# A 512-column matmul over both halves of the activations in three wide up projections

## The chip, the cores and the metric

The program runs on one core of a Trainium2 chip. Its time is the device time of one execution in microseconds (us). TensorE (PE in the profile) multiplies, ScalarE (ACT) and VectorE (DVE) do the elementwise work, GpSimd (POOL) does a few small powers and loads, and the DMA queue of SyncE (SP) brings in the weights.

## The reference, cut to what matters

Two blocks of a transformer, for 256 tokens of width 1024, in float32. Three of their layers are wide; they are the ones that change.

```python
def squared_relu_mlp(h, w_up, w_down):          # w_up 1024 x 4096, w_down 4096 x 1024, once
    return jnp.square(jax.nn.relu(h @ w_up)) @ w_down

def conv_ffn(h, up, conv_w, conv_b, down):      # up 1024 x 5632, down 2816 x 1024, in two layers
    u = causal_depthwise_conv(h @ up, conv_w, conv_b)      # width 3, along the tokens
    g, val = jnp.split(u, 2, axis=-1)
    return (jax.nn.silu(g) * val) @ down
```

## The kernel before, in words

**Split numbers.** Each float32 matrix is kept as two float32r matrices, a high half (the value rounded, `whi`, `h_hi`, `r_hi`) and a low half (the value minus the high half, `wlo`, `h_lo`, `r_lo`). A product is three matmuls into one PSUM region: high by high, high by low, low by high (`three`, L1860 to L1862).

**Units.** The weights come in 203 units of at most 1 MB in the order of use, through five slots. SyncE loads unit u once unit u-5 has been used. ScalarE makes its high half (`hi()`, L737), VectorE its low half (`lo()`, L1144), and TensorE waits for the low half in `weights(u)`.

**Wide layers.** The hidden dimension is cut into groups of 256 columns, 16 in the squared-ReLU layer (called MLP below) and 11 in each convolution layer (FFN below). An MLP group has one up unit (1024 x 256) and one down unit (256 x 1024). An FFN group has two up units, x = 0 for the gate and x = 1 for the value, and one down unit. The up product is made transposed, with the weights as the stationary operand and the activations as the moving one: for each of 2 column blocks c and 8 row blocks k, three matmuls with 256 columns (the tokens). Both column blocks of a unit share one PSUM bank. A down unit is 24 matmuls with 512 columns, with the activations stationary; it accumulates over all groups into banks 4 to 7.

**Order on TensorE.** In the MLP: up 0, up 1, down 0, up 2, down 1, and so on to down 15. In each FFN: group 0's up product in another form with the tokens on the partitions (`first_half`, `first_back`), then both units of up 1, down 0, up 2, down 1, ..., up 9, up 10, down 8, and downs 9 and 10 together (`last_two_wide`: for each of 4 output banks first the 6 matmuls of down 9, then the 6 of down 10). So the up units of groups 9 and 10 follow each other, four in a row. TensorE waits for `up_lo` (MLP) or `f_lo` (FFN) of the group before its down unit; both are given by VectorE's subtraction that makes `r_lo` (L1536, L1715).

**Order on ScalarE and VectorE.** Their programs are written out by hand, and each engine takes its instructions in that order. For an FFN group g of 1 or more:

```python
# ScalarE
hi(); ffn_first(g, 0)    # 2 Identity with scale and bias (L998), then Copy to the padded buffer (L1000)
hi(); ffn_first(g, 1)
ffn_silu(g); hi(); ffn_part(g)          # L1004, L737, L1008: r_hi
# VectorE
lo(); ffn_taps(g, 0)     # waits for the Copy, then 4 scalar_tensor_tensor (L1701)
lo(); ffn_taps(g, 1)
ffn_prod(g); lo(); ffn_part(g)          # L1710, L1144, L1715: r_lo, gives f_lo
```

Group 0 has no `hi()` in it and only the first two `lo()`. For an MLP group ScalarE does Relu (L900), Square (L902) and the high half (L904), VectorE only `r_lo` (L1536), each with its `hi()` or `lo()` around it.

**Banks.** A bank may be written again only when it has been drained; here that is the inc that ScalarE's reading instruction gives. Up units turn through banks 0, 1, 2 (MLP) and 0 to 3 (FFN).

Of the kernel before, what the change touches and what calls it, by code (L numbers as in the profile page):

```python
# [33 lines left out]
F32 = mybir.dt.float32  # L34
F32R = mybir.dt.float32r
# [172 lines left out]
def plan(w):  # L208
# [100 lines left out]
    def mlp_up(g):  # L309
        p.unit(("up", g), w["w_up"][0], 0, KD, 256 * g, 256)  # L310
        p.gemm(("up", g), ("up", g), g % 3)

# [53 lines left out]
    def ffn(layer, name, sum_banks, first_banks):  # L366
        p.tile_transposes(name, sum_banks)
        up, down = w["ffn_up_2"][layer], w["ffn_down_2"][layer]

        def ffn_up(g):  # L370
            for x in range(2):
                p.unit(("fu", layer, g, x), up, 0, KD, FFN * x + 256 * g, 256)
                if g:
                    p.gemm(("fu", layer, g, x), ("fu", layer, g, x), 2 * (g % 2) + x)
# [73 lines left out]
def build(nc, w, out):  # L448
# [3 lines left out]
    with ctx:  # L452
# [10 lines left out]
        whi = [sb(f"whi{i}", [P, UNIT], F32R) for i in range(SLOTS)]  # L463
        h_hi, h_lo = sb("h_hi", [P, KD, T], F32R), sb("h_lo", [P, KD, T], F32R)
        r_hi, r_lo = sb("r_hi", [P, KD, T], F32R), sb("r_lo", [P, KD, T], F32R)
# [83 lines left out]

        bank = [ctx.enter_context(nc.psum_tensor(f"bank{i}", [P, 512], F32)) for i in range(8)]  # L550

# [21 lines left out]
        xa_max, xa_p, up_sq = sem("xa_max"), sem("xa_p"), sem("up_sq")  # L573
        f_conv, f_silu, f_prod = (sem(n) for n in ("f_conv", "f_silu", "f_prod"))
        dt_log, dta_ready, cum_row = sem("dt_log"), sem("dta_ready"), sem("cum_row")
# [144 lines left out]
        def _(act):  # L720
# [267 lines left out]
            def ffn_first(layer, g, x):  # L988

                p_ = g % 2  # L990
                key = ("fu", layer, g, x)
                b = wait_bank(act, key)
                if x == 0 and g >= 2:
                    act.wait_ge(f_lo, 11 * layer + g - 1)
                for ct in range(2):
                    tile = FFN_TILES * x + 2 * g + ct
                    wcol, bcol = 128 + 132 * layer + 88 + tile, 392 + 44 * layer + tile
                    A(fcv[p_][x][:, ct, :], b[:, T * ct:T * ct + T], ACT.Identity, scale=pv[:, wcol:wcol + 1],  # L998
                      bias=pv[:, bcol:bcol + 1])
                A(fpad[p_][x][:, :, 2:2 + T], pair(b), ACT.Copy).then_inc(drained[use[key][0]], 1)  # L1000

# [124 lines left out]
        def _(dve):  # L1126
            V = nc.vector
            steps, parts, nxt, powers = [0], [0], [0], [0]

            def mark(ins):  # L1130
# [562 lines left out]
            def ffn_taps(layer, g, x):  # L1693
                key = ("fu", layer, g, x)
# [149 lines left out]
        def _(pe):  # L1844
# [350 lines left out]
            def mlp_first():  # L2195

                w_hi, w_lo, kt, n = weights(at[("up", 0)])
                b = claim(("up", 0))
                for half in range(2):
                    for c in range(2):  # L2200
                        for k in range(4 * half, 4 * half + 4):
                            if c == 0 and k % 2 == 0:
                                wait_drained(pe, ("h3", k // 2))
                            cs = slice(P * c, P * c + P)
                            last = three(b[:, T * c:T * c + T], w_hi[:, k, cs], w_lo[:, k, cs], h_hi[:, k, :], h_lo[:, k, :],
                                         (c, k) == (0, 0), (c, k) == (1, kt - 1))
                        if (half, c) == (0, 0):
# [3 lines left out]
            def mlp_up(g):  # L2211
                if g == 0:
                    mlp_first()
                else:
                    b_unit(at[("up", g)], h_hi, h_lo, one(("up", g)))

# [125 lines left out]
            def ffn(layer, name, before_last):  # L2342
# [46 lines left out]
                for n, (what, g) in enumerate(FFN_ORDER):  # L2389
                    if what == "up":  # L2390
                        for x in range(2):
                            key = ("fu", layer, g, x)
                            b_unit(at[key], h_hi, h_lo, one(key), between=up_second if (g, x) == (1, 0) else None)
                    elif g < FFN_GROUPS - 2:
# [191 lines left out]
```

## Time and profile before

| | |
|---|---|
| time, median of 3 runs | 1349.54 us (1348.79 to 1351.38) |
| the profiled execution | 1347.98 us, span 1346.2 us |
| TensorE busy | 1294.0 us, 96% of the span |
| VectorE busy | 884.4 us, 66% |
| ScalarE busy | 675.5 us, 50% |
| chain that ended last | TensorE 86%, VectorE 7%, ScalarE 3% |
| mean granted TensorE clock | 0.994 |
| HBM read | 219.91 MB |

A busy share says how much of the span an engine worked; the chain says which work set the end. The durations of single instructions include their latency, and neighbours overlap, so the cost of one more instruction is read from the distance of the starts of two neighbours. The unit boundaries are seen on SyncE's queue: it issues a load as soon as TensorE has finished a unit.

### The profile page before, as it was taken

What the parts mean: (1) busy time and instruction counts of PE and PEld (TensorE: products, weight loads), DVE (VectorE), ACT (ScalarE), POOL (GpSimd) and SP (SyncE); (2) the same over time, 40 slices, a digit from 0 to 9 for tenths busy, and PEclk for the clock granted to TensorE, in tenths of its full rate; (3) what the DMA queues carried; (4) which work ended last, traced back from release to release, by engine and by line L of the source; (5) the groups of instructions that cost most, each with busy time, mean ns of one, the idle gap of its engine ahead of it and who ended that gap; (6) DMA issues with size and microseconds to landing.
All of it is one profiled execution on the core that took longest, in us unless ns stands there. A gap on an engine that the chain in (4) does not pass through costs nothing.

```text
span 1346.2 us, 20023 instructions
## 1 busy us (share of the span) xinstructions
PE 1294.0 (96%) x8543; PEld 1177.6 (87%) x8543; DVE 884.4 (66%) x1174; ACT 675.5 (50%) x844; POOL 53.8 (4%) x62
## 2 busy tenths in 40 slices
PE   6999999999999999989999999899999899899997
PEld 6878999988979999989998777899998877899996
DVE  5665757775446444467876777676668757676667
ACT  3555434444435444446674443455555463555552
POOL 4000000100000000000000000000000100000000
PEclk9999999999999999989999999999999999999999
DMA  9644555655435555545552233555554532555551
GB/s 338 196 125 132 182 157 169 226 184 197 163 94 185 188 188 188 164 142 179 168 183 95 94 116 113 179 188 188 188 188 135 179 126 94 188 175 185 184 184 56
DMA packets 155241, 222.26 MB, mean 165 GB/s; under 512 B 4997, under 2 KB 117377, under 8 KB 155024
## 3 DMA queue, kind: packets, MB, share of 16 engines
q1 hardware_dynamic: 151936, 210.38, 48.2%
q0 software_dynamic: 2928, 10.00, 2.0%
q8 instruction: 68, 1.11, 0.3%
q10 hardware_dynamic: 288, 0.59, 0.1%
q14 instruction: 21, 0.17, 0.0%
HBM read 219.91 MB, written 1.05 MB: 164 GB/s over the span
## 4 chain that ended last, share of the span: by engine, by line
PE 86%; DVE 7%; ACT 3%; issue 2%; DMA 1%; POOL 1%; POOLq 0%; DVEq 0%; SPq 0%; ACTq 0%
PE bank L1860 26%; PE bank L1861 26%; PE bank L1862 26%; DVE wlo L1144 1%; ACT whi L737 1%; DMA raw<-in_w_in 1%; POOL rstd L646 1%; PE bank L2280 1%; PE bank L2281 1%; PE bank L2140 1%; PE bank L1952 1%; PE bank L2027 0%; PE bank L2161 0%; DVE bn L1260 0%; ACT h_hi L746 0%
## 5 line engine op out<-in xcount | busy, mean ns | idle before, releaser
L1144 DVE TENSOR_TENSOR wlo<-raw,whi 128x2048 fp32r<-128x2048 f32 (+2 forms) x203 | 454.3, 2247 | 120.5 <-ACT whi L737 120.1
L1860 PE MATMUL bank<-h_hi,whi 128*128 128x256 f32 x1568 | 448.5, 286 | 8.2 <-DVE wlo L1144 5.1
L1861 PE MATMUL bank<-h_lo,whi 128*128 128x256 f32 x1568 | 446.2, 285 | 0.0
L1862 PE MATMUL bank<-h_hi,wlo 128*128 128x256 f32 x1568 | 446.1, 285 | 0.0
L737 ACT ACTIVATE whi<-raw 128x2048 fp32r<-128x2048 f32 (+2 forms) x203 | 379.2, 1881 | 25.4 <-DMA raw<-in_w_in 12.8
L1860 PEld LDWEIGHTS bank<-h_hi,whi 128*128 128x128 f32 x1568 | 303.5, 194 | 11.1 <-DVE wlo L1144 8.5
L1861 PEld LDWEIGHTS bank<-h_lo,whi 128*128 128x128 f32 x1568 | 303.6, 194 | 1.2
L1862 PEld LDWEIGHTS bank<-h_hi,wlo 128*128 128x128 f32 x1568 | 303.4, 194 | 0.0
L1860 PE MATMUL bank<-whi,r_hi 128*128 128x512 f32 (+1 forms) x464 | 180.1, 388 | 3.9 <-DVE wlo L1144 1.4
L1861 PE MATMUL bank<-wlo,r_hi 128*128 128x512 f32 (+1 forms) x464 | 178.3, 384 | 0.0
L1862 PE MATMUL bank<-whi,r_lo 128*128 128x512 f32 (+1 forms) x464 | 178.0, 384 | 0.0
L1701 DVE SCALAR_TENSOR_TENSOR arena<-arena,pv 128x256 f32<-128x256 f32 x176 | 77.5, 482 | 96.8 <-ACT arena L1000 95.2
L1860 PE MATMUL bank<-whi,h_hi 128*128 128x512 f32 (+4 forms) x320 | 117.0, 366 | 1.3 <-issue 0.9
L1861 PE MATMUL bank<-wlo,h_hi 128*128 128x512 f32 (+4 forms) x320 | 114.2, 357 | 0.0
L1862 PE MATMUL bank<-whi,h_lo 128*128 128x512 f32 (+4 forms) x320 | 114.2, 357 | 0.0
L1860 PEld LDWEIGHTS bank<-whi,r_hi 128*128 128x128 f32 x464 | 87.4, 188 | 20.9 <-issue 3.5
L754 ACT ACTIVATE arena<-bank 128x512 f32<-128x512 f32 (+3 forms) x81 | 43.3, 558 | 122.8 <-PE bank L1862 109.5
L998 ACT ACTIVATE arena<-bank,pv 128x256 f32<-128x256 f32 x88 | 44.9, 562 | 117.5 <-PE bank L1862 112.5
L1862 PEld LDWEIGHTS bank<-whi,r_lo 128*128 128x128 f32 x464 | 87.2, 188 | 17.6
L1861 PEld LDWEIGHTS bank<-wlo,r_hi 128*128 128x128 f32 x464 | 87.4, 188 | 15.1
L1860 PEld LDWEIGHTS bank<-whi,h_hi 128*128 128x128 f32 x320 | 60.8, 190 | 10.2 <-issue 2.6
L1862 PEld LDWEIGHTS bank<-whi,h_lo 128*128 128x128 f32 x320 | 60.9, 190 | 8.5
(296 smaller groups left out, 1356.1 us busy)
## 6 DMA issues: line engine op xcount, KB each, us to landing
raw<-in_ffn_up SPq DMA_DIRECT2D x44, 1024.0 KB, 5.1
raw<-in_w_in SPq DMA_DIRECT2D x32, 1024.0 KB, 5.8
raw<-in_ssd_in_proj SPq DMA_DIRECT2D x24, 1024.0 KB, 5.4
raw<-in_ffn_down SPq DMA_DIRECT2D x22, 1024.0 KB, 4.9
raw<-in_w_up SPq DMA_DIRECT2D x16, 1024.0 KB, 5.4
raw<-in_w_down SPq DMA_DIRECT2D x16, 1024.0 KB, 4.8
raw<-in_w_xkv SPq DMA_DIRECT2D x8, 1024.0 KB, 5.1
raw<-in_ssd_out_proj SPq DMA_DIRECT2D x8, 1024.0 KB, 5.0
```

What stands on the lines that cost most here:

```text
L646: nc.gpsimd.tensor_tensor(rstd[:, t:t + 1], ms[:, t:t + 1], mhalf[:, t:t + 1], ALU.pow).then_inc(rstd_ready, 1)
L737: A(whi[u % SLOTS][:, 0:kt * n], raw[u % SLOTS][:, 0:kt * n], ACT.Copy).then_inc(hi_split, 1)
L754: A(dst, src(b), ACT.Copy).then_inc(drained[use[key][0]], 1)
L998: A(fcv[p_][x][:, ct, :], b[:, T * ct:T * ct + T], ACT.Identity, scale=pv[:, wcol:wcol + 1], bias=pv[:, bcol:bcol + 1])
L1144: V.tensor_tensor(wlo[s][:, 0:kt * n], raw[s][:, 0:kt * n], whi[s][:, 0:kt * n].bitcast(F32), ALU.subtract).then_inc(lo_split, 1)
L1701: ins = V.scalar_tensor_tensor(y, fpad[g % 2][x][:, ct, tap:tap + T], pv[:, wcol:wcol + 1], y, ALU.mult, ALU.add)
L1860: M(o, a_hi, b_hi, start=start, stop=False)
L1861: M(o, a_hi, b_lo, start=False, stop=False)
L1862: return M(o, a_lo, b_hi, start=False, stop=stop_)
L1952: last = nc.tensor.transpose(b[:, P * k:P * k + P], xn[:, t, P * (4 * c + k):P * (4 * c + k) + P], ident)
L2140: last = M(b[:, T * t:T * t + T], qT[:, 2 * i + kk, P * t:P * t + P], kT[:, 2 * i + kk, :], start=kk == 0, stop=kk == 1)
L2280: M(b[:, 0:TRI], pick[:, h:h + 1].to_broadcast([2 * SSD_HEADS, P]), crow2[:, :], start=True, stop=False)
```

## The change

In the up units of the three layers (all 16 in the MLP, those of groups 1 to 10 in each FFN) the two halves of the activations lie behind each other in one buffer `h_both`, and a matmul with the high half of the weights takes both, as 512 columns: columns 0 to 255 of the bank get high by high, columns 256 to 511 high by low. The third product, low by high, stays a 256-column matmul into columns 0 to 255. Each column block now fills a bank of its own, two banks per unit. ScalarE copies the upper half of both banks out (`low_copy`), VectorE adds the lower half of each bank to it (`add_halves`) and gives the banks free. In the FFN, ScalarE's Identity instructions come after that and read SBUF; VectorE's taps wait for them (`f_last`). In the MLP, ReLU and square are one `scalar_tensor_tensor` on VectorE. Group 0 of each FFN keeps its product; there ScalarE copies first and its Identity instructions read the copy.

```diff
+            def both(b, w_hi_k, w_lo_k, k, kt):          # TensorE
+                if k == 0:
+                    M(b[:, :], w_hi_k, h_both[:, :, k, :], start=True, stop=False)
+                    return M(b[:, 0:T], w_lo_k, h_hi[:, k, :], start=False, stop=False)
+                M(b[:, 0:T], w_lo_k, h_hi[:, k, :], start=False, stop=False)
+                return M(b[:, :], w_hi_k, h_both[:, :, k, :], start=False, stop=k == kt - 1)
...
+            def low_copy(dst, keys):                      # ScalarE
+                b0 = use[keys[0]][0]
+                for key in keys:
+                    wait_bank(act, key)
+                A(dst, psum[:, b0:b0 + 2, T:2 * T], ACT.Copy).then_inc(low_out, 1)
...
             def mlp_group(g):
-                A(up_r[g % 3], pair(b), ACT.Relu).then_inc(drained[g % 3], 1)
-                wait_drained(act, key)
-                A(up_s[g % 3], up_r[g % 3], ACT.Square).then_inc(up_sq, 1)
+                low_copy(up_r[g % 3], [("up", g, c) for c in range(2)])
                 act.wait_ge(up_sq, g + 1)
                 A(r_hi[:, 2 * (g % 3):2 * (g % 3) + 2, :], up_s[g % 3], ACT.Copy).then_inc(x_hi, 1)
...
             def ffn_first(layer, g, x):
-                b = wait_bank(act, key)
+                if g == 0:
+                    b = wait_bank(act, ("fu", layer, 0, x))
+                    A(fpad[p_][x][:, :, 2:2 + T], pair(b), ACT.Copy).then_inc(drained[use[("fu", layer, 0, x)][0]], 1)
+                    wait_drained(act, ("fu", layer, 0, x))
+                else:
+                    keys = [("fu", layer, g, x, c) for c in range(2)]
+                    low_copy(fpad[p_][x][:, :, 2:2 + T], keys)
+                    for key in keys:
+                        wait_drained(act, key)
                 for ct in range(2):
-                    A(fcv[p_][x][:, ct, :], b[:, T * ct:T * ct + T], ACT.Identity, ...)
-                A(fpad[p_][x][:, :, 2:2 + T], pair(b), ACT.Copy).then_inc(drained[use[key][0]], 1)
+                    ins = A(fcv[p_][x][:, ct, :], fpad[p_][x][:, ct, 2:2 + T], ACT.Identity, ...)
+                ins.then_inc(f_last, 1)
...
+            def add_halves(dst, pad, keys):               # VectorE
+                lows[0] += 1
+                dve.wait_ge(low_out, lows[0])
+                for c, key in enumerate(keys):
+                    b, y = wait_bank(dve, key), dst[:, c, pad:pad + T]
+                    V.tensor_tensor(y, y, b[:, 0:T], ALU.add).then_inc(done(key), 1)
...
             def mlp_part(g):
+                add_halves(up_r[g % 3], 0, [("up", g, c) for c in range(2)])
+                V.scalar_tensor_tensor(up_s[g % 3], up_r[g % 3], 0.0, up_r[g % 3], ALU.max, ALU.mult).then_inc(up_sq, 1)
...
             def ffn_taps(layer, g, x):
-                wait_drained(dve, key)
+                if g:
+                    add_halves(fpad[g % 2][x], 2, [("fu", layer, g, x, c) for c in range(2)])
+                dve.wait_ge(f_last, 22 * layer + 2 * g + x + 1)
```

The plan gives MLP group g the banks 2(g % 2) and 2(g % 2) + 1, and an FFN unit x the banks 2(1 - x) and 2(1 - x) + 1.

## Rows read from the trace of the kernel before

**Rows 1.** The page: busy time of the engines, and the chain that ended last.

```profile
PE 1294.0 (96%) x8543; PEld 1177.6 (87%) x8543; DVE 884.4 (66%) x1174; ACT 675.5 (50%) x844; POOL 53.8 (4%) x62
...
PE 86%; DVE 7%; ACT 3%; issue 2%; DMA 1%; POOL 1%; POOLq 0%; DVEq 0%; SPq 0%; ACTq 0%
```

**Rows 2.** Timeline of TensorE at unit boundaries: start, duration, engine, line, operation.

```profile
891.10 0.28 PE L1862 MATMUL bank<-h_hi,wlo 128*128 128x256 f32 x1
891.22 0.40 PE L1860 MATMUL bank<-whi,r_hi 128*128 128x512 f32 x1
...
896.46 0.39 PE L1862 MATMUL bank<-whi,r_lo 128*128 128x512 f32 x1
896.68 0.28 PE L1860 MATMUL bank<-h_hi,whi 128*128 128x256 f32 x1
```

**Rows 3.** Timeline of SyncE's queue: loads issued when a unit ends.

```profile
902.63 0.37 SPq L623 DMA_DIRECT2D raw<-in_ffn_down  x1
908.39 5.83 SPq L623 DMA_DIRECT2D raw<-in_ffn_up  x2
```

**Rows 4.** Timeline of ScalarE, last two groups of the first FFN.

```profile
1004.52 1.02 ACT L998 ACTIVATE arena<-bank,pv 128x256 f32<-128x256 f32 x2 [4.61 <-PE bank L1862]
1005.43 0.59 ACT L1000 ACTIVATE arena<-bank 128x512 f32<-128x512 f32 x1
1005.91 1.92 ACT L737 ACTIVATE whi<-raw 128x2048 fp32r<-128x2048 f32 x1
```

**Rows 5.** Timeline of VectorE in the same stretch.

```profile
1006.06 1.80 DVE L1701 SCALAR_TENSOR_TENSOR arena<-arena,pv 128x256 f32<-128x256 f32 x4 [3.62 <-ACT arena L1000]
...
1014.33 2.29 DVE L1144 TENSOR_TENSOR wlo<-raw,whi 128x2048 fp32r<-128x2048 f32 x1
...
1017.13 2.28 DVE L1144 TENSOR_TENSOR wlo<-raw,whi 128x2048 fp32r<-128x2048 f32 x1
1019.34 1.79 DVE L1701 SCALAR_TENSOR_TENSOR arena<-arena,pv 128x256 f32<-128x256 f32 x4
1021.04 2.28 DVE L1144 TENSOR_TENSOR wlo<-raw,whi 128x2048 fp32r<-128x2048 f32 x1
1023.34 1.80 DVE L1701 SCALAR_TENSOR_TENSOR arena<-arena,pv 128x256 f32<-128x256 f32 x4
...
1025.86 1.75 DVE L1144 TENSOR_TENSOR wlo<-raw,whi 128x1536 fp32r<-128x1536 f32 x1
1027.53 0.68 DVE L1715 TENSOR_TENSOR r_lo<-arena,r_hi 128x512 fp32r<-128x512 f32 x1
```

**Rows 6.** Timeline of TensorE: first matmul that needs the last group's `r_lo`.

```profile
1028.43 0.40 PE L1860 MATMUL bank<-whi,r_hi 128*128 128x512 f32 x1
```

**Rows 7.** Timelines of VectorE: additions from PSUM of 384 and of 512 columns.

```profile
801.40 0.55 DVE L1673 TENSOR_TENSOR crow<-crow,bank 128x384 f32<-128x384 f32 x1
...
402.43 1.28 DVE L1505 TENSOR_TENSOR xn<-xn,bank 128x512 f32<-128x512 f32 x2
```

**Rows 8.** Timelines at the MLP's start: VectorE, then TensorE's first down matmul.

```profile
412.45 2.29 DVE L1144 TENSOR_TENSOR wlo<-raw,whi 128x2048 fp32r<-128x2048 f32 x1
414.66 0.68 DVE L1536 TENSOR_TENSOR r_lo<-arena,r_hi 128x512 fp32r<-128x512 f32 x1
...
416.22 0.40 PE L1860 MATMUL bank<-whi,r_hi 128*128 128x512 f32 x1
```

**Rows 9.** Timeline of VectorE at the first FFN's start.

```profile
871.73 2.29 DVE L1144 TENSOR_TENSOR wlo<-raw,whi 128x2048 fp32r<-128x2048 f32 x1 [1.11 <-ACT whi L737]
```

**Rows 10.** TensorE's longest pauses: timelines, then windows (us; busy; PEclk third from last).

```profile
587.94 1.44 PE L1973 MATMUL bank<-cst,xn 128*128 128x128 f32 x6 [3.57 <-DVE xn L1225]
866.79 0.38 PE L1860 MATMUL bank<-h_hi,whi 128*128 128x256 f32 x1 [2.55 <-DVE wlo L1144]
...
868.00:871.30 3.30, 3.30 (x18) 3.30 (x17) 1.82 (x4) 2.03 (x2) 0.00 (x0) 0.50 0.22 82
1166.70:1172.00 5.30, 5.25 (x43) 5.25 (x44) 3.35 (x7) 2.76 (x3) 0.00 (x0) 1.00 0.35 145
```

More of the change, by code:

```diff
@@ L310, in mlp_up @@
         p.unit(("up", g), w["w_up"][0], 0, KD, 256 * g, 256)
-        p.gemm(("up", g), ("up", g), g % 3)
+        for c in range(2):
+            p.gemm(("up", g, c), ("up", g), 2 * (g % 2) + c)
     def mlp_down(g):
@@ L373, in ffn_up @@
                 if g:
-                    p.gemm(("fu", layer, g, x), ("fu", layer, g, x), 2 * (g % 2) + x)
+                    for c in range(2):
+                        p.gemm(("fu", layer, g, x, c), ("fu", layer, g, x), 2 * (1 - x) + c)
         def ffn_down(g):
@@ L548, in build @@
         ftN = room(8192, NT, 512)
-        bank = [ctx.enter_context(nc.psum_tensor(f"bank{i}", [P, 512], F32)) for i in range(8)]
+        psum = ctx.enter_context(nc.psum_tensor("psum", [P, 8, 512], F32))
+        bank = [psum[:, i, :] for i in range(8)]
         landed = [sem(f"landed{i}") for i in range(SLOTS)]
@@ L573, in build @@
         xa_max, xa_p, up_sq = sem("xa_max"), sem("xa_p"), sem("up_sq")
-        f_conv, f_silu, f_prod = (sem(n) for n in ("f_conv", "f_silu", "f_prod"))
+        f_conv, f_silu, f_prod, f_last = (sem(n) for n in ("f_conv", "f_silu", "f_prod", "f_last"))
+        low_out = sem("low_out")
         dt_log, dta_ready, cum_row = sem("dt_log"), sem("dta_ready"), sem("cum_row")
@@ L997, in ffn_first @@
                     wcol, bcol = 128 + 132 * layer + 88 + tile, 392 + 44 * layer + tile
-                    A(fcv[p_][x][:, ct, :], b[:, T * ct:T * ct + T], ACT.Identity, scale=pv[:, wcol:wcol + 1],
-                      bias=pv[:, bcol:bcol + 1])
-                A(fpad[p_][x][:, :, 2:2 + T], pair(b), ACT.Copy).then_inc(drained[use[key][0]], 1)
+                    ins = A(fcv[p_][x][:, ct, :], fpad[p_][x][:, ct, 2:2 + T], ACT.Identity, scale=pv[:, wcol:wcol + 1],
+                            bias=pv[:, bcol:bcol + 1])
+                ins.then_inc(f_last, 1)
             def ffn_silu(layer, g):
@@ L1533, in mlp_part @@
             def mlp_part(g):
+                add_halves(up_r[g % 3], 0, [("up", g, c) for c in range(2)])
+                for c in range(2):
+                    wait_drained(dve, ("up", g, c))
+                V.scalar_tensor_tensor(up_s[g % 3], up_r[g % 3], 0.0, up_r[g % 3], ALU.max, ALU.mult).then_inc(up_sq, 1)
+                dve.wait_ge(up_sq, g + 1)
                 s = slice(2 * (g % 3), 2 * (g % 3) + 2)
@@ L1883, in b_unit, with both_unit @@
                         last = three(o, w_hi[:, k, cs], w_lo[:, k, cs], x_hi_[:, tile0 + k, :], x_lo_[:, tile0 + k, :], k == 0, k == kt - 1)
+                last.then_inc(unit_used, 1)
+            def both(b, w_hi_k, w_lo_k, k, kt):
[4 more added lines that the diff above has]
+                return M(b[:, :], w_hi_k, h_both[:, :, k, :], start=False, stop=k == kt - 1)
+            def both_unit(u, keys, between=None):
+                w_hi, w_lo, kt, _ = weights(u)
+                for c in range(2):
+                    b = claim(keys[c])
+                    if between is not None:
+                        between(c)
+                    for k in range(kt):
+                        cs = slice(P * c, P * c + P)
+                        last = both(b, w_hi[:, k, cs], w_lo[:, k, cs], k, kt)
                 last.then_inc(unit_used, 1)
@@ L2197, in mlp_first @@
                 w_hi, w_lo, kt, n = weights(at[("up", 0)])
-                b = claim(("up", 0))
+                b = [claim(("up", 0, c)) for c in range(2)]
                 for half in range(2):
@@ L2204, in mlp_first @@
                             cs = slice(P * c, P * c + P)
-                            last = three(b[:, T * c:T * c + T], w_hi[:, k, cs], w_lo[:, k, cs], h_hi[:, k, :], h_lo[:, k, :],
-                                         (c, k) == (0, 0), (c, k) == (1, kt - 1))
+                            last = both(b[c], w_hi[:, k, cs], w_lo[:, k, cs], k, kt)
                         if (half, c) == (0, 0):
@@ L2214, in mlp_up @@
                 else:
-                    b_unit(at[("up", g)], h_hi, h_lo, one(("up", g)))
+                    both_unit(at[("up", g)], [("up", g, c) for c in range(2)])
             def mlp_down(g):
@@ L2391, in ffn @@
                         for x in range(2):
-                            key = ("fu", layer, g, x)
-                            b_unit(at[key], h_hi, h_lo, one(key), between=up_second if (g, x) == (1, 0) else None)
+                            both_unit(at[("fu", layer, g, x)], [("fu", layer, g, x, c) for c in range(2)],
+                                      between=up_second if (g, x) == (1, 0) else None)
                     elif g < FFN_GROUPS - 2:
```

8 lines of the change are left out of this document (3 added, 5 removed).

## The prediction

> **What bounds the kernel now.** I read the page first: TensorE is busy for 96% of the span and is 86% of the chain that ended last, VectorE 7% and ScalarE 3% [rows 1]. So a shorter stream on TensorE is worth its full length, as long as nobody keeps TensorE waiting. Next the timeline of TensorE, for what one matmul costs: a 256-column one to the next start 0.12 us (891.10 to 891.22), a 512-column one 0.22 to 0.23 (896.46 to 896.68) [rows 2]. Then SyncE's queue: an up unit of 48 matmuls takes 908.39 - 902.63 = 5.76 us, so 0.120 each; the second load of the pair starts at 908.39 + 5.83 - 0.37 = 913.85, so a down unit of 24 takes 5.46, 0.2275 each [rows 3]. Last ScalarE and VectorE in one FFN group and at the starts and ends of the layers, for how far ahead of TensorE they are.
>
> **What TensorE gains.** Per column block and k, 3 x 0.120 = 0.360 us become one 512- and one 256-column matmul. The two kinds alternate, and just these two transitions are in the trace: 0.12 and between 0.22 and 0.2275 [rows 2, 3]. I take 0.1200 + 0.2265 = 0.3465, so 0.0135 saved, x 16 = 0.21 us a unit (5.76 to 5.55). Bounds: 0.2 (with 0.2275) and 0.3 (with 0.22); below, nothing, if the moving operand in two pieces streams worse, which no row shows. The number of columns stays 768; what goes is one instruction's fixed part, 0.120 - 256/2400 = 0.013 us. There are 16 + 2 x 20 = 56 such units, 11.8 us if all of it counted.
>
> The Trainium skill ("TensorE: Matmul & The Clock Gate", "Wait — 56ns, not 53.3ns?") gives a warm matmul a fixed part of about 2.5 ns, not 13. By it a unit would gain 0.04 us, the 56 units 2.2. The rows of this kernel show 13 ns at both sizes, so I go by them.
>
> **What a hand-over costs.** Before, from the end of an FFN up unit to VectorE's taps: two Identity and a Copy on ScalarE, 1004.52 to 1006.06, 1.54 us [rows 4, 5]. After: Copy 0.59 [rows 4]; two additions of 256 columns from PSUM; the two Identity, 1.02 from PSUM [rows 4], taken as 1.07 from SBUF; three signals between engines of 0.03 to 0.04 each. An addition of that size is not in the trace. 384 columns take 0.55, 512 take 0.68 with 0.60 from start to start (two in 1.28) [rows 7], so 0.42 and 0.34 on that line, 0.76 for the pair; bounds 0.6 (twice half of the 0.60) and 1.1 (twice the 0.55). Sum 0.59 + 0.76 + 1.07 + 0.10 = 2.5 us. Two things are worse than the 1.0 more: VectorE stands in its queue between the additions and the taps while ScalarE does the Identity pair (0.76 + 1.1 = 1.9 us of VectorE's time per unit that were not there), and ScalarE stands before them while VectorE finishes a low half (2.29 us [rows 5]); the next `hi()` is queued behind it.
>
> **FFN, steady state.** Set the end of unit (g, 0) to 0. ScalarE copies to 0.6, VectorE adds to 1.4, taps from 2.5, low half 4.3 to 6.6. Unit (g, 1) ends at 5.55; adds 6.5 to 7.3, taps 8.4 (1.9 with the wait for its end), product 10.3 to 10.9, low half 10.9 to 13.2, `r_lo`, low half 13.7 to 16.0. The next (g + 1, 0) ends at 2 x 5.55 + 5.46 = 16.6 and its additions begin at 17.2. So VectorE keeps up, with 1.2 us to spare in 16.6; the low half for the unit at 16.6 - 5.55 = 11.0 is there at 6.6, the one for 16.6 at 13.2, the group's `r_lo` (13.8) is wanted at 22. Banks of unit (g, 0) are wanted at 11.0 and free at 1.4. Nothing waits: the gain counts.
>
> **FFN, end.** Groups 9 and 10 give TensorE four up units in a row without a down unit between, and VectorE's queue does not get shorter. Before, with the end of (9, 0) at 1004.5: product of group 9 done, low half at 1014.33, another at 1017.13, taps of (10, 0) at 1019.34, low half 1021.04, taps of (10, 1) 1023.34, low half 1025.86, last `r_lo` 1027.53 to 1028.21 [rows 5], and TensorE wants it at 1028.43 [rows 6]. It was ready 0.2 us in time, with VectorE busy nearly without a break from 1013.7. The change puts the additions and the wait for Identity into this very stretch. From the end of (9, 0): low half 10.9 (before 9.8), `r_lo`, low half 13.7 to 16.0, additions of (10, 0) 15.9, taps 17.8 (before 14.8), low half 19.6 to 21.9, additions of (10, 1) 21.8, taps 23.7 (before 18.8), low half 26.2 to 27.9, `r_lo` to 28.6. That is 1.1 + 1.9 + 1.9 = 4.9 us later than 23.7. TensorE wants it after 3 x 5.55 + 5.46 + 6 x 0.2275 = 23.5. Stall: 5.1 us. The second FFN is the last layer and has no weights left for that last low half (1.75 from 1025.86, of which 0.9 then remains as the path over ScalarE's `r_hi`): 4.2 us. Each of the three hand-overs in the stretch carries the pair's price: at 0.6 the stalls are 4.7 and 3.8, at 1.1 they are 6.0 and 5.1.
>
> **FFN, start.** Here VectorE is what TensorE waits for already (2.55 us at 866.79 [rows 10]), and its queue is full until 880. Up to the low half of down 0, 871.73 to 874.02 [rows 9], the order changes little (+0.1). Then additions to 874.8, Identity to 875.9, and only then ScalarE's next `hi()` (1.92 [rows 4]) to 877.7; low half of unit (2, 0) 877.7 to 880.0 where TensorE is free at 879.9; additions 879.9, taps 881.8, product, low half of (2, 1) 884.3 to 886.6, start 886.65 instead of 885.6. So the gain of the units before it is lost, and 1.0 us more, in each FFN: +2.1. The 17 later units gain 17 x 0.21 = 3.6 each, 7.1 for both.
>
> **MLP.** VectorE has the time: per group 11 us, of which two low halves, `r_lo`, and now additions and the square. At the start it has not: `r_lo` of group 0 came at 414.66 behind a low half [rows 8]; now additions to 415.4, square 0.7 to 416.1, ScalarE's high half 0.63 to 416.8, `r_lo` to 417.5, and down 0 starts at 417.56 instead of 416.22: +1.3. The 14 units behind it gain 2.9.
>
> **The clock.** The one pause of more than 3.5 us inside the run, 3.57 to 587.94, and one of the two of 2.55 us, to 866.79, were followed by a granted clock of 0.50, that is 1.2 GHz: 3.3 us in the window from 868.0; behind the other 2.55 us pause, from 1166.7, it stayed 1.00 [rows 10]. Stalls of 5.1 and 4.2 us should each bring that, and behind them lie 42 matmuls of TensorE's own work: as long as behind 866.79, half of some 3.3 us is lost, 1.7 each, +3.4; bounds 0 and 3.4 each. For the 1.5 us pause in the MLP I take nothing.
>
> **Sum.** -7.1 - 2.9 + 2.1 + 1.3 + 5.1 + 4.2 + 3.4 = +6.1 us. On the profiled execution, 1347.98 (span 1346.2 and 1.8 around it), 1354.1. That execution is 1.6 below the median of 1349.54, within the spread of the runs; I forecast 1355.
>
> **Rivals.**
> - The stalls at the ends don't come, for instance because VectorE passes the hand-overs much faster than I think; it decides if the last `r_lo` is there 23.5 us after (9, 0), and everything above that counts one for one. For it: 4.9 us to spare in mid-layer before. Against it: [rows 5, 6]. Then -7.1 - 2.9 + 3.4 (starts) = -6.6: 1343, faster. 0.13.
> - The stalls come and the clock stays up, as behind the pause at 1166: +2.7, 1352. 0.2.
> - The 512-column matmul over two pieces costs what the two it replaces cost. Then the 48 gaining units give nothing (+10.1), the stalls shrink by 0.4 each as TensorE comes later: 1365. For it only that no row shows such an operand; against it the 13 ns in [rows 2, 3]. 0.05. The skill's 2.5 ns lies near this case.
> - VectorE becomes the bound in mid-layer: the 1.2 us to spare are gone if a hand-over takes 0.6 more. At 1.0 more each, 0.8 x 9 groups x 2 layers = +14, and as much in the ends as 2: 1370. 0.05.
> - My forecast: 0.57.
>
> **Range and chances.** 0.2% is 2.7 us, about what a measurement of this kernel can tell from no change. My case lies above it with its addition bounds (-0.8, +1.8) and with one clock drop missing (-1.7); the second rival lies on the edge and is shared. Slower 0.73, same 0.13, faster 0.14. The range goes down to the first rival and up by the upper bounds of additions and clock: 1343 to 1362; the likeliest case alone 1351 to 1359.
>
> **What would show it.** Per step: start-to-start pairs of 0.12 and 0.226 in the up units and a steady FFN period of 16.6 instead of 17.0 us; the pair of additions 0.76, the taps 2.5 us after a unit's end; TensorE idle before the down 10 half of the last pair, 5 us in the first and 4 in the second FFN, released by VectorE's L1715, each followed by 1.2 GHz; 1.5 us idle before down 0 of the MLP. It is wrong if TensorE's pauses there are under 2 us, if the period is above 17, or if the clock stays at 1.00 behind the pauses.

## The result, and the profile after

The changed kernel takes 1363.22 us (median of 4 runs, 1359.71 to 1363.92) against 1349.40 for the kernel before, timed beside it: a ratio of 1.0096, 95% interval 1.0080 to 1.0111, so 13.8 us slower. 1355 was forecast, 5.6 more than before. The sign and the place were right, the size was not: the time lies 1.2 us above the range. The profiled execution is 1362.54 us with a span of 1360.4, 14.2 longer than the span before.

The page of the profile first: the busy times, and the chain of work that ended last.

```profile
PE 1293.5 (95%) x7647; PEld 1132.6 (83%) x7647; DVE 936.2 (69%) x1302; ACT 672.6 (49%) x828; POOL 53.7 (4%) x62
...
PE 80%; DVE 11%; ACT 4%; issue 3%; DMA 1%; POOL 1%; POOLq 0%; DVEq 0%; SPq 0%; ACTq 0%
```

TensorE's busy time did not fall although 896 instructions went [rows 1]; VectorE has 52 us more work; and the chain moved 6 points from TensorE, 4 of them to VectorE. Now the stream on TensorE (start, duration, engine, line, operation), in an up unit of FFN group 2, up to the first down matmul:

```profile
892.00 0.40 PE L1922 MATMUL psum<-h_both,whi 128*128 128x512 f32 x1
892.24 0.28 PE L1921 MATMUL psum<-h_both,wlo 128*128 128x256 f32 x1
892.35 0.40 PE L1922 MATMUL psum<-h_both,whi 128*128 128x512 f32 x1
892.58 0.40 PE L1890 MATMUL psum<-whi,r_hi 128*128 128x512 f32 x1
```

From 892.00 to 892.35 a 512-column and a 256-column matmul take 0.35, where three times 0.12 stood [rows 2]. SyncE's queue gives the unit more exactly: 909.42 - 903.83 = 5.59 us, against 5.76 [rows 3]. The down unit behind it takes 5.81 - 0.37 = 5.44.

```profile
903.83 0.37 SPq L628 DMA_DIRECT2D raw<-in_ffn_down  x1
909.42 5.81 SPq L628 DMA_DIRECT2D raw<-in_ffn_up  x2
```

So the saving is there, 0.17 us a unit. What it costs is seen on ScalarE and VectorE in the last two groups of the first FFN; the first two rows answer to [rows 4]:

```profile
1003.65 0.60 ACT L906 ACTIVATE arena<-psum 128x512 f32<-128x512 f32 x1 [2.98 <-PE psum L1922]
1005.12 1.09 ACT L1013 ACTIVATE arena<-arena,pv 128x256 f32<-128x256 f32 x2 [0.87 <-DVE arena L1184]
```

VectorE in the same stretch, answering to [rows 5] (taps are L1731, additions L1184, `r_lo` L1745):

```profile
1004.29 0.75 DVE L1184 TENSOR_TENSOR arena<-arena,psum 128x256 f32<-128x256 f32 x2 [1.08 <-ACT arena L906]
1006.25 1.80 DVE L1731 SCALAR_TENSOR_TENSOR arena<-arena,pv 128x256 f32<-128x256 f32 x4 [1.21 <-ACT arena L1013]
...
1019.75 0.75 DVE L1184 TENSOR_TENSOR arena<-arena,psum 128x256 f32<-128x256 f32 x2
1021.71 1.80 DVE L1731 SCALAR_TENSOR_TENSOR arena<-arena,pv 128x256 f32<-128x256 f32 x4 [1.21 <-ACT arena L1013]
...
1025.73 0.74 DVE L1184 TENSOR_TENSOR arena<-arena,psum 128x256 f32<-128x256 f32 x2
1027.70 1.79 DVE L1731 SCALAR_TENSOR_TENSOR arena<-arena,pv 128x256 f32<-128x256 f32 x4 [1.22 <-ACT arena L1013]
...
1031.88 0.69 DVE L1745 TENSOR_TENSOR r_lo<-arena,r_hi 128x512 fp32r<-128x512 f32 x1
```

One hand-over from start of the additions to start of the taps takes 1.96 us of VectorE's time, 1.2 of it idle. The `r_lo` that TensorE wants comes at 1031.88 to 1032.57, where it came at 1027.53 before. TensorE's pauses, with what ended them: the ends of both FFN layers, down 0 of the MLP, and the two at the start of the first FFN.

```profile
1032.61 0.80 PE L1890 MATMUL psum<-whi,r_hi 128*128 128x512 f32 x1 [5.47 <-DVE r_lo L1745]
...
1340.34 0.80 PE L1890 MATMUL psum<-whi,r_hi 128*128 128x512 f32 x1 [4.59 <-DVE r_lo L1745]
...
416.92 0.47 PE L1890 MATMUL psum<-whi,r_hi 128*128 128x512 f32 x1 [1.68 <-DVE r_lo L1565]
...
866.91 0.68 PE L1919 MATMUL psum<-h_both,whi 128*128 128x512 f32 x1 [2.81 <-DVE wlo L1160]
...
886.88 0.50 PE L1919 MATMUL psum<-h_both,whi 128*128 128x512 f32 x1 [0.82 <-DVE wlo L1160]
```

Last the windows at 1.2 GHz that the kernel before did not have, but for a fifth in the start-up, at 17.1 to 20.6 us, behind which the unit boundaries lie no later than before (us; busy time of PE, PEld, DVE, ACT, POOL; granted clock third from last):

```profile
1030.90:1037.70 6.80, 5.09 (x12) 4.07 (x13) 4.71 (x5) 1.43 (x2) 0.00 (x0) 0.50 0.00 0
1338.10:1344.90 6.80, 4.56 (x11) 3.59 (x12) 2.77 (x5) 0.63 (x1) 0.00 (x0) 0.50 0.00 0
1123.10:1126.40 3.30, 3.30 (x12) 2.80 (x12) 3.10 (x7) 1.36 (x5) 0.00 (x0) 0.50 0.00 0
744.20:747.50 3.30, 3.30 (x10) 2.64 (x10) 0.55 (x1) 2.35 (x3) 0.00 (x0) 0.50 0.46 179
```

Half of TensorE's busy time in a window is what the clock cost: 2.5 and 2.3 us behind the two long pauses, 1.65 in each of the other two, where SyncE's queue shows a step of 1.6 us from one unit boundary to the next.

### The profile page after: what moved, and what is told of

The parts are those of the page before. It is cut to its first block, busy times and chain, and to the rows that moved or that the text cites. A ratio compares the mean times of both kernels' runs of the same rounds, so it can differ in the third digit from the quotient of the medians.

```text
span 1360.4 us, 18512 instructions
## 1 busy us (share of the span) xinstructions
PE 1293.5 (95%) x7647; PEld 1132.6 (83%) x7647; DVE 936.2 (69%) x1302; ACT 672.6 (49%) x828; POOL 53.7 (4%) x62
## 3 DMA queue, kind: packets, MB, share of 16 engines
HBM read 219.91 MB, written 1.05 MB: 162 GB/s over the span
## 4 chain that ended last, share of the span: by engine, by line
PE 80%; DVE 11%; ACT 4%; issue 3%; DMA 1%; POOL 1%; POOLq 0%; DVEq 0%; SPq 0%; ACTq 0%
PE psum L1890 18%; PE psum L1891 18%; PE psum L1892 18%; PE psum L1922 11%; PE psum L1921 5%; DVE wlo L1160 3%; DVE arena L1731 2%; PE psum L1919 2%; ACT whi L742 1%; ACT arena L1013 1%; PE psum L1920 1%; DMA raw<-in_w_in 1%; POOL rstd L651 1%; PE psum L2329 1%; DVE arena L1184 1%
## 5 line engine op out<-in xcount | busy, mean ns | idle before, releaser
L1922 PE MATMUL psum<-h_both,whi 128*128 128x512 f32 x784 | 280.8, 397 | 0.0
L1921 PE MATMUL psum<-h_both,wlo 128*128 128x256 f32 x784 | 219.8, 280 | 0.3 <-DVE h_both L1192 0.3
L1890 PE MATMUL psum<-whi,r_hi 128*128 128x512 f32 (+1 forms) x464 | 182.7, 394 | 15.7 <-DVE r_lo L1745 10.1
L1890 PE MATMUL psum<-h_both,whi 128*128 128x256 f32 x672 | 193.9, 289 | 2.7 <-DVE h_both L1172 2.7
L1891 PE MATMUL psum<-h_both,whi 128*128 128x256 f32 x672 | 192.4, 286 | 0.0
L1892 PE MATMUL psum<-h_both,wlo 128*128 128x256 f32 x672 | 192.3, 286 | 0.0
L1891 PE MATMUL psum<-wlo,r_hi 128*128 128x512 f32 (+1 forms) x464 | 180.1, 388 | 0.0
L1892 PE MATMUL psum<-whi,r_lo 128*128 128x512 f32 (+1 forms) x464 | 180.0, 388 | 0.0
L1922 PEld LDWEIGHTS psum<-h_both,whi 128*128 128x128 f32 x784 | 148.2, 189 | 30.2
L1921 PEld LDWEIGHTS psum<-h_both,wlo 128*128 128x128 f32 x784 | 148.6, 190 | 5.8 <-DVE h_both L1192 0.6
L1890 PEld LDWEIGHTS psum<-h_both,whi 128*128 128x128 f32 x672 | 131.3, 195 | 3.8 <-DVE wlo L1160 2.7
L1892 PEld LDWEIGHTS psum<-h_both,wlo 128*128 128x128 f32 x672 | 131.2, 195 | 0.0
L1891 PEld LDWEIGHTS psum<-h_both,whi 128*128 128x128 f32 x672 | 131.1, 195 | 0.0
L1731 DVE SCALAR_TENSOR_TENSOR arena<-arena,pv 128x256 f32<-128x256 f32 x176 | 77.5, 482 | 65.0 <-ACT arena L1013 63.4
L1890 PE MATMUL psum<-whi,h_both 128*128 128x512 f32 (+4 forms) x320 | 117.5, 367 | 1.2 <-issue 0.9
L1891 PE MATMUL psum<-wlo,h_both 128*128 128x512 f32 (+4 forms) x320 | 114.5, 358 | 0.0
L1892 PE MATMUL psum<-whi,h_both 128*128 128x512 f32 (+4 forms) x320 | 114.3, 357 | 0.0
```

Of the source, the lines that this page charges most:

```text
L1890: M(o, a_hi, b_hi, start=start, stop=False)
L1891: M(o, a_hi, b_lo, start=False, stop=False)
L1892: return M(o, a_lo, b_hi, start=False, stop=stop_)
L1921: M(b[:, 0:T], w_lo_k, h_hi[:, k, :], start=False, stop=False)
L1922: return M(b[:, :], w_hi_k, h_both[:, :, k, :], start=False, stop=k == kt - 1)
```

## Experiments

Each was timed beside the kernel before on the same chip. The medians of the kernel before were 1350.55 for the first four experiments, 1350.59 for the next three and 1350.30 for the last two, where it was 1349.40 beside the changed kernel. So a distance between a version and the changed kernel (1363.22) carries about 1 us of this.

**The new form in the MLP alone.** In the edits with `FFN_OLD` and `MLP_OLD` these name the groups that keep three 256-column matmuls and ScalarE's old instructions. The banks stay in the changed kernel's plan, and group 0 of each FFN keeps the changed order (Copy, then Identity).

```diff
+FFN_OLD = (1, 2, 3, 4, 5, 6, 7, 8, 9, 10)
+MLP_OLD = ()
```

> The changed form in the MLP only; both FFNs as before. Theory (the new matmul pair gains 0.17 us a unit wherever VectorE is not late, and only the first down of the MLP waits): TensorE loses 1.9 us once before down 0 and gains 14 x 0.165 = 2.3, so 0.5 to 0.9 us under the kernel before, 1348.7. Rival (the pair of matmuls or the second bank costs time wherever it is used, and the layers' ends are a side effect): at or above 1349.4.

Measured: 1348.56, ratio 0.9990 (0.9981 to 0.9999). The pause before down 0 is there:

```profile
418.06 0.47 PE L1913 MATMUL psum<-whi,r_hi 128*128 128x512 f32 x1 [1.68 <-DVE r_lo L1586]
```

So the MLP is not where the time went; it wins 1.4 us by the ratio (0.1 to 2.6 by the interval, 2.0 between the medians), hardly to be told from nothing. On SyncE's queue TensorE loses 1.9 us at down 0 and gains 2.6 over the 14 units behind it.

**The last two FFN groups in the old form.**

```diff
+FFN_OLD = (9, 10)
+MLP_OLD = ()
```

> The changed kernel, with groups 9 and 10 of both FFNs in the form of before. Theory (the loss is VectorE's lateness in the four up units at the end of each FFN): the pauses of 5.5 and 4.6 us and the half clock behind them (2.6 and 2.3) go, 15.0 us, and 8 units lose 0.17 each, 1.4: 13.6 us under the changed kernel, 1349.6. Rival (the loss is spread over all units): 8 of 56 units undone gives back a seventh, 2 us: 1361.

Measured: 1345.02, ratio 0.9961 (0.9948 to 0.9973), 18.2 under the changed kernel where 13.6 was expected. Four of 36 FFN and MLP groups undone turn a loss of 13.8 us into a gain of 5.5. The window over the stretch in which TensorE paused:

```profile
1015.00:1035.00 20.00, 19.69 (x106) 16.75 (x105) 17.81 (x24) 8.34 (x11) 1.53 (x1) 1.00 0.36 110
```

TensorE is busy for 19.69 of 20 us at the full clock. In the profiled executions, the pauses (10.1), the half clock behind them (4.8) and the windows at 744 and 1123 (3.2) are gone; against that stand 8 units without their gain (1.3). That is 16.8 of the 17.0 us between the spans. One more window at half clock came, at the start of the second FFN (1166.3 to 1169.7), and it cost nothing: TensorE comes 1.6 us later out of it, but a little further on VectorE is late anyway, and the pause of 1.52 us that the changed kernel has there, up to 1182.95, is gone.

**The new form only where VectorE has time.** MLP groups 1 to 15, FFN groups 3 to 8.

```diff
+FFN_OLD = (1, 2, 9, 10)
+MLP_OLD = (0,)
```

> The new form only where VectorE is ahead: MLP groups 1 to 15 and FFN groups 3 to 8; MLP group 0 and FFN groups 1, 2, 9 and 10 as before. Theory: no stall is added, 15 + 24 = 39 units gain 0.165 each, 6.4 us under the kernel before: 1343.0, with FFN periods of 16.6 in the middle. Rival (the new form costs as much elsewhere as it gains): 1349.

Measured: 1340.51, ratio 0.9929 (0.9915 to 0.9942): 10.0 us faster than before, and the best of all. SyncE's queue shows the unit of 5.6 us, and the windows at both FFN ends the full clock without a pause:

```profile
892.60 0.37 SPq L635 DMA_DIRECT2D raw<-in_ffn_up  x1
898.18 0.37 SPq L635 DMA_DIRECT2D raw<-in_ffn_down  x1
```

```profile
1010.00:1030.00 20.00, 20.00 (x111) 17.38 (x109) 17.79 (x24) 9.09 (x12) 1.53 (x1) 1.00 0.36 112
1310.00:1330.00 20.00, 19.81 (x101) 16.64 (x100) 14.53 (x23) 4.45 (x6) 1.53 (x1) 1.00 0.03 10
```

39 units of 0.165 us are 6.4, and 27 down units between them, at 5.44 for 5.47, another 0.8: 7.2, where the interval says 7.8 to 11.5 and the two profiled executions differ by 8.3. Unit by unit on SyncE's queue, 7.0 of the 8.3 lie in the MLP (2.7) and the FFN groups (2.1 in each layer), less 0.5 at the two FFN starts, where group 0 keeps the changed order. The other 1.8 are not in the new form: 1.0 in the start-up, before the first wide layer, which differed by as much (0.8) between two executions of the changed kernel, and 0.8 between 583 and 609 us, where both kernels fall to half clock twice, but not at the same places. The timed executions may differ further by the clock: its mean was 0.992 or 0.993 in this kernel's and 0.989 to 0.993 in those of the kernel before. That part is not shown. What the run shows firmly is that the matmul part of the change is worth having, some 6.5 us net in the traces, and the hand-over in three places (MLP group 0, the FFN starts and the FFN ends) is not.

**TensorE kept busy through the pauses.** The changed kernel, with matmuls in the pause whose result nobody reads: 23 in the first FFN, 19 in the second, into an idle bank. VectorE is exactly as late as before; only the pause as such, and what follows from it for the clock, is taken away.

```diff
+                    if i:                                  # before down 10's half of the last pair
...
+                        for n in range((23, 19)[layer]):
+                            M(bank[2][:, :], h_hi[:, 0, 0:P], w_hi[:, 0, 0:512], start=True, stop=True)
```

> The changed kernel; TensorE runs 23 (first FFN) and 19 (second) extra 512-column matmuls into an idle bank where it would wait for the last r_lo. Output unchanged. Theory (the pause, not the wait as such, brings the clock down to 1.2 GHz): the pause shrinks below 0.5 us at the same length of the stall, the granted clock stays 1.00 behind it, 2.6 + 2.3 = 4.9 us under the changed kernel, 1358.3. Rival (the clock falls for another reason, or the matmuls only take the place of the pause): no change, 1363.

Measured: 1356.41, ratio 1.0047 (1.0035 to 1.0060), 6.8 under the changed kernel; about 5 was expected. TensorE at the first end, then the clock there:

```profile
1025.34 5.37 PE L2455 MATMUL psum<-whi,h_both 128*128 128x512 f32 x23
1030.99 0.50 PE L1890 MATMUL psum<-whi,r_hi 128*128 128x512 f32 x1 [0.28 <-DVE r_lo L1745]
```

```profile
1024.00:1034.00 10.00, 9.72 (x43) 7.75 (x42) 8.41 (x13) 5.01 (x6) 0.00 (x0) 1.00 0.21 66
1050.40:1053.70 3.30, 3.30 (x12) 3.30 (x11) 3.30 (x4) 0.57 (x1) 0.00 (x0) 0.50 0.88 303
```

The real work starts as late as ever (1030.99 for 1032.61, but everything behind 744 lies 1.6 us earlier here, as the fall at 744 did not come), and the clock behind it stays at 1.00. The second end is the same: 1.00 from 1328 to 1338. So the fall behind the long pauses comes from TensorE's standing still, not from the late VectorE. By the unit boundaries it was worth 2.4 us at the first end and 2.2 at the second, near the 4.8 that the windows of the changed kernel show; the absent fall at 744 makes 1.6 of the 6.2 us between the profiled spans. The waits themselves remain: this kernel is 11.4 us above the one with the last two groups in the old form. A fall at 1050 came instead, in a stretch that is the same in both kernels (the last section comes back to it).

**One run of 512 contiguous columns.** Is the missing part of the gain (0.17 for 0.21 a unit) the price of an operand in two pieces?

```diff
-        h_both = sb("h_both", [P, 2, KD, T], F32R)
-        h_hi, h_lo = h_both[:, 0], h_both[:, 1]
+        h_both = sb("h_both", [P, KD, 2, T], F32R)
+        h_hi, h_lo = h_both[:, :, 0], h_both[:, :, 1]
...
-                return M(b[:, :], w_hi_k, h_both[:, :, k, :], start=False, stop=k == kt - 1)
+                return M(b[:, :], w_hi_k, h_both[:, k, :, :], start=False, stop=k == kt - 1)
```

> The changed kernel with h_both laid out [k][half][token], so that the 512 moving columns lie in one piece instead of two 8 KB apart. Output unchanged. Theory A (the two pieces make the 512-column matmul take 0.233 instead of 0.2265 us from start to start): the pair falls from 0.349 to 0.3465 or less, 5.55 us a unit, 2 us less in all. Theory B (the alternation of 512 and 256 columns has this price whatever the layout): 0.349 stays, no change.

Measured: 1362.15, ratio 1.0087 (1.0073 to 1.0101), the same as the changed kernel.

```profile
909.10 0.27 PE L1921 MATMUL psum<-h_both,wlo 128*128 128x256 f32 x1
909.22 0.40 PE L1922 MATMUL psum<-h_both,whi 128*128 128x512 f32 x1
909.45 0.28 PE L1921 MATMUL psum<-h_both,wlo 128*128 128x256 f32 x1
```

0.35 for the pair as before (0.12 and 0.23): the layout is not the cause.

**The Identity pair on VectorE.** If the hand-over is dear because VectorE stands while ScalarE works, it should be cheaper for VectorE to do that work itself.

```diff
-                if x == 0 and g >= 2:                      # ScalarE: its two ACT.Identity go, and this wait
-                    act.wait_ge(f_lo, 11 * layer + g - 1)
...
+                    for ct in range(2):                    # VectorE
...
+                        ins = V.tensor_scalar(fcv[g % 2][x][:, ct, :], fpad[g % 2][x][:, ct, 2:2 + T],
+                                              pv[:, wcol:wcol + 1], pv[:, bcol:bcol + 1], ALU.mult, ALU.add)
```

> The changed kernel with the Identity pair of FFN groups 1 to 10 on VectorE (two tensor_scalar of 256 columns, about 0.31 each from start to start) instead of on ScalarE between the additions and the taps. Theory (VectorE's standing while ScalarE does Identity is a part of its lateness): additions to taps 1.56 instead of 1.97 us, three times in the last four units, 1.2 us less stall in each FFN, something like 0.6 less at each start, 4 us in all: 1359. Rival (VectorE is bound by its own work, so more work for it makes it later): 1363 or above.

Measured: 1354.32, ratio 1.0033 (1.0022 to 1.0044), 8.9 under the changed kernel and more than the 4 expected. VectorE, then TensorE's pauses, then the clock behind them:

```profile
1016.26 0.75 DVE L1181 TENSOR_TENSOR arena<-arena,psum 128x256 f32<-128x256 f32 x2
1017.12 0.73 DVE L1728 TENSOR_SCALAR arena<-arena,pv 128x256 f32<-128x256 f32 x2
1017.89 1.80 DVE L1737 SCALAR_TENSOR_TENSOR arena<-arena,pv 128x256 f32<-128x256 f32 x4
```

```profile
1028.34 0.50 PE L1896 MATMUL psum<-whi,r_hi 128*128 128x512 f32 x1 [3.97 <-DVE r_lo L1751]
...
1332.59 0.80 PE L1896 MATMUL psum<-whi,r_hi 128*128 128x512 f32 x1 [3.08 <-DVE r_lo L1751]
```

```profile
1028.90:1032.20 3.30, 3.30 (x9) 2.54 (x8) 2.19 (x3) 0.00 (x0) 0.00 (x0) 0.50 0.00 0
```

Additions to taps take 1.63 instead of 1.96, with more work on VectorE. Each pause is 1.5 shorter. There are four such hand-overs between the end of (9, 0) and the last `r_lo`, each 0.33 to 0.35 cheaper, which is 1.35 of it; in neither trace does VectorE wait for a high half in this stretch. The stretch at half clock behind the first is 3.4 us where it was 6.8. That the gain is more than 4 has three more causes in the profiled executions, 8.3 us apart: 1.4 less half clock, 0.8 less at each FFN start, and 1.6 for the fall at 744, which did not come here and has nothing to do with the edit.

**The kernel before, with VectorE made late.** The opposite test: no new matmul form at all, only 8 extra additions of 512 columns in VectorE's queue before the taps of (9, 1), (10, 0) and (10, 1), results unread.

```diff
+                for n in {(9, 1): (0, 1), (10, 0): (2, 3, 4), (10, 1): (5, 6, 7)}.get((g, x), ()):
+                    V.tensor_tensor(spare[n], pv[:, 0:512], pv[:, 0:512], ALU.add)
```

> The kernel before, matmuls and banks untouched, with 8 extra additions of 512 columns on VectorE (0.60 us each, 4.8 in all: 2 before the taps of unit (9, 1), 3 each before those of (10, 0) and (10, 1)) in both FFNs. Output unchanged. Theory (VectorE's lateness alone makes the pauses and the half clock): TensorE idles 4.6 us in the first and 3.7 in the second FFN, each followed by a granted clock of 0.50 that costs about 2.3: 13 us over the kernel before, 1362. Rival (the stall belongs to the new matmul form or its banks): within 2 us of 1349.4.

Measured: 1361.75, ratio 1.0080 (1.0067 to 1.0093); 1362 was expected.

```profile
1029.95 0.79 PE L1863 MATMUL bank<-whi,r_hi 128*128 128x512 f32 x1 [4.38 <-DVE r_lo L1718]
...
1337.71 0.50 PE L1863 MATMUL bank<-whi,r_hi 128*128 128x512 f32 x1 [3.50 <-DVE r_lo L1718]
```

```profile
1028.30:1035.00 6.70, 5.05 (x12) 3.99 (x13) 4.64 (x5) 1.36 (x1) 0.00 (x0) 0.50 0.00 0
1338.90:1342.20 3.30, 3.30 (x10) 2.55 (x9) 1.38 (x2) 0.00 (x0) 0.00 (x0) 0.50 0.00 0
1120.40:1123.70 3.30, 3.30 (x12) 2.83 (x12) 3.15 (x7) 1.36 (x5) 0.00 (x0) 0.50 0.00 0
```

Lateness of VectorE alone, with the old stream on TensorE, makes both pauses and the half clock behind them: 7.9 us of waiting lengthened the time by 11.2. At the first end the unit boundary moves by 7.0, of which the pause is 4.4 and the half clock 2.5. It is no copy of the changed kernel, whose pauses are longer and which has the later starts and the gains besides.

**The changed kernel once more.** Do the falls at 744 and at 1123 belong to the change?

> The changed kernel as it is, beside the next one. Theory (where the clock falls after short pauses in the rest of the run differs from run to run, the two pauses at the FFNs' ends always bring it down): both pauses of 5.5 and 4.6 us again followed by 6.8 us at 0.50; short falls elsewhere in other places than in the first profile; 12 to 13 us over the kernel before. Rival (the falls at 744 and 1123 belong to the change): they come again in the same stages.

Measured: 1362.87, ratio 1.0097 (1.0082 to 1.0113), 12.6 over the kernel before.

```profile
741.00:750.00 9.00, 7.53 (x40) 5.91 (x39) 5.07 (x10) 3.40 (x6) 0.00 (x0) 1.00 0.35 117
1028.90:1035.60 6.70, 5.16 (x12) 4.11 (x13) 4.54 (x5) 1.25 (x1) 0.00 (x0) 0.50 0.00 0
1121.10:1124.40 3.30, 3.30 (x11) 2.83 (x12) 3.23 (x7) 1.36 (x5) 0.00 (x0) 0.50 0.00 0
```

The fall at 744 did not come again, behind a pause of the same length (1.44 for 1.46 us). It had come with the contiguous layout, at 745.2 behind 1.43 us, and in no other of the eleven profiled executions, all of which have this pause (1.43 to 1.46 us): it is a matter of the single execution. The one near 1121 came again. It does not belong to the new form either, for the kernel with only a late VectorE has it too.

**The best version, with the matmuls sorted.** The last candidate for the missing part of the gain was the turning from 512 to 256 columns and back. Per column block: one 512-column matmul, then eight of 256, then seven of 512.

```diff
+                    M(b[:, :], w_hi[:, 0, cs], h_both[:, :, 0, :], start=True, stop=False)
+                    for k in range(kt):
+                        M(b[:, 0:T], w_lo[:, k, cs], h_hi[:, k, :], start=False, stop=False)
+                    for k in range(1, kt):
+                        last = M(b[:, :], w_hi[:, k, cs], h_both[:, :, k, :], start=False, stop=k == kt - 1)
```

> As e3_slack_only, and in the units of the new form the matmuls of a column block are sorted: one of 512 columns, the 8 of 256, the other 7 of 512, instead of one of each in turn. Output unchanged. Theory (taking turns between 512 and 256 columns is what makes the pair 0.3497 instead of 0.3465): 5.54 us a unit instead of 5.59, 36 to 39 units, 2 us under e3_slack_only, 11 us under the kernel before. Rival (each 512-column matmul over the activations costs 0.233 in any order): 5.59 a unit, as e3_slack_only, 9 to 10 under the kernel before.

Measured: 1340.58, ratio 0.9927 (0.9915 to 0.9940), the same as unsorted.

```profile
909.24 0.39 PE L1955 MATMUL psum<-h_both,whi 128*128 128x512 f32 x1
909.47 1.11 PE L1957 MATMUL psum<-h_both,wlo 128*128 128x256 f32 x8
910.42 1.78 PE L1959 MATMUL psum<-h_both,whi 128*128 128x512 f32 x7
912.04 0.39 PE L1955 MATMUL psum<-h_both,whi 128*128 128x512 f32 x1
```

A block takes 912.04 - 909.24 = 2.80, the unit 5.59 as ever. Eight of 256 take 0.95 (0.119 each), seven of 512 take 1.62 (0.231 each), where the 512-column matmuls of down units take 0.227. The order is not the cause either. (The profiled execution is 1.2 us longer than the unsorted kernel's; a half-clock stretch of 6.8 us at the start of the second FFN, from 1160 on, makes up 1.1 of it.) But the surplus is not in every one of them. By the distances of the starts in the 20 column blocks behind 905 us, the 512-column matmuls of row blocks 0, 6 and 7 take 0.227, as those of down units do, and those of row blocks 1 to 5 take 0.228 to 0.236. So the moving operand as such is not the cause, and what is stays open.

## Why the prediction was right about the way and short in size

The terms of the sum against the profiled execution of the changed kernel. Measured shifts are the differences between the two traces in the place of the same unit boundary.

| Step | forecast, us | measured, us |
|---|---|---|
| MLP: start +1.3, 14 units -2.9 | -1.6 | -0.9 |
| Starts of the two FFN layers | +2.1 | +3.1 |
| 34 FFN units with slack, and the down units between them | -7.1 | -5.6 |
| Pauses at the ends | +9.3 | +10.1 |
| Half clock behind them | +3.4 | +4.8 |
| Half clock at 744 and 1123 | 0 | +3.2 |
| Start-up (-1.0) and rest | 0 | -0.5 |
| Sum | +6.1 | +14.2 |

The profiled execution of the kernel before had a mean clock of 0.994, its later timed ones 0.989 to 0.993: the table is set against an execution with few falls.

**The gain per unit** was mis-sized: 5.76 to 5.59, not to 5.55. I put a 512-column matmul over the activations at 0.2265, by [rows 2, 3], where the 512 moving columns are weights; it takes 0.234, and the 256-column one in turn with it 0.116 instead of 0.120. Over 48 units the missing 0.045 us are 2.2. The table shows 1.5 in the FFNs and 0.7 in the MLP, where a dearer start and down units at 5.44 for 5.47 are in it too. The fixed part that a dropped matmul gives back is thus 0.360 - 0.350 = 0.010 us; 0.0135 was assumed. The Trainium skill's 2.5 ns ("TensorE: Matmul & The Clock Gate", "Wait — 56ns, not 53.3ns?") would make a unit's gain 0.04 us; the trace shows 0.17, so the measurement decides against it here.

**The hand-over** came out as worked out: additions 0.75 to 0.76 for the pair (forecast 0.76), Identity 1.09 (1.07), taps at 1006.25, 2.6 us after ScalarE's copy starts at 1003.65, just behind the unit's end (2.5). The last `r_lo` is done 28.9 us after the copy's start (28.6 after the unit's end). A group in mid-layer takes 2 x 5.59 + 5.44 = 16.62 (16.6). The pauses of 5.5 and 4.6 (5.1 and 4.2) follow from it. This was the step that carried the sign, and the late-VectorE run shows it alone is enough.

**FFN starts.** Low half of (2, 0) from 877.85 (forecast 877.7), unit (2, 1) from 886.88 (886.65). The shift over this stretch is 1.4 and 1.7 us, where 1.05 each was forecast. In the first FFN it has two parts that I left out: group 0, where ScalarE's Identity now comes behind the Copy, hands over 0.12 later, so the first pause ends at 866.91 instead of 866.79; and the start of (2, 1) was set against 885.6 before, where [rows 2, 3] give 891.22 - 5.76 = 885.46. In the second layer 0.36 more come still before the first up unit: a wait for VectorE, up to 1157.96, is 1.32 us long instead of 0.97. Why is open.

**MLP.** The pause is 1.7 us where 1.5 was forecast, and the start costs 1.8 where 1.3 was. The 14 units behind it, with their down units, gain 2.6 where 2.9 was forecast.

**The clock** is the step that failed most, and the gain per unit the next. The forecast took the length of the half-clock stretch from the one behind a pause of 2.55 us [rows 10] and carried it to pauses twice as long: 3.3 us, 1.7 lost each. Behind the long ones it lasted 6.8 us, part of it while TensorE still waited, and cost 2.5 and 2.3. The upper bound of 3.4 each would have covered that. But I let the clock fall only in those two places. Both profiles of the changed kernel show one more fall at 1121 to 1123, and one of them a second at 744, behind a pause of 1.46 us that was 1.44 long before and brought none. So of the gap of 8.1 us to the forecast shift, 4.6 are clock (1.4 behind the pauses, 3.2 elsewhere), 2.2 the smaller gain, 1.0 the starts and 0.8 the pauses, less 0.5 of start-up and rest. The 1.6 at 744 are chance of the single execution.

Rival by rival: the stalls came, so the first is out; the clock fell, so is the second; the 512-column matmul is dearer than I took it but far cheaper than two; and mid-layer VectorE kept up, with no pause of TensorE over 0.1 us between 887 and 1027.

## What to carry to other kernels

A saving on the bounding engine that is paid for with work on another must be priced where that other engine has no slack, not on the average: here VectorE, busy for 66% of the span, was late at the ends of the two FFNs (8 of the 56 units), and that alone took 15 us where the units with slack gave 8. Where slack differs from group to group, apply the form per group: with it in 39 of the 56 units the kernel is 0.7% faster than before, with it in all 56 it is 1.0% slower. And a long wait of the matrix engine can be charged twice, once as idle time and once as the half clock behind it: behind each of the ten pauses of 3.0 to 5.5 us at the FFN ends the second bill was 1.7 to 2.6 us.

## What the runs showed of the hardware that I had not expected

How long TensorE stays at half clock behind a pause, and whether it falls at all, is not a function of the pause alone. At the FFN ends it was 6.8 us each time behind 5.5 and 4.6 us (the changed kernel twice, the contiguous layout), 6.8 behind 4.38, and 3.4 behind 3.97, 3.50 and 3.08. But behind the pause of 3.57 to 3.73 us at 584 to 588, which all eleven profiled executions have, it was 3.4 in eight and 6.8 in three. Behind the first FFN's start (2.55 to 2.81 us) all eleven fell for 3.4 us; behind the same pause at the second FFN's start nine did not fall, the kernel with the last two groups in the old form did for 3.4 us and the sorted one for 6.8. Behind the 1.43 to 1.46 us at 740 to 745 two of eleven fell. The Trainium skill ("TensorE: Matmul & The Clock Gate", "What's actually happening") has the slow level as the default, released by recent activity, and the chip's look at that activity as free-running, not tied to the kernel's start; the traces agree in that the same pause is followed by a fall in one execution and not in another.

A fall can come without a long pause ahead of it. The four executions in which the pause at the first FFN's end was followed by 6.8 us at half clock (the changed kernel twice, the contiguous layout, the late VectorE) all fell again near 1121 to 1124, behind pauses of about 1 us. Three others (MLP alone, filled, Identity on VectorE) fell once at 1046 to 1050, and the rest in neither place. With one profile of each that may be chance or a phase set by the first fall; it is not settled, and it is worth 1.6 us each time.

And a matmul of 512 columns does not have one price: in the up units it takes 0.234 us from start to start in turn with 256-column ones, in one piece or in two, and 0.231 in a row of seven, but in the down units, with weights as the moving operand, 0.227. In the sorted kernel those of row blocks 0, 6 and 7 have the price of the down units with the same kind of operands, so neither the kind of the moving operand nor its layout explains the difference.
